# Output projection and tokens cut to 520 columns, w_out in sixteen single blocks split on GpSimd, a tenth expert weight buffer, and rows stored unscaled

## The reference, cut to what matters

```python
xn   = rmsnorm(x, norm_mix);  z, xbc, dt, u = split(xn @ w_in)
y_ssd = rmsnorm(ssd(conv(xbc), dt) * silu(z), ssd_norm)      # state-space heads, chunks of 128
y_s5  = s5(u); y_s5 = rmsnorm(gelu(y_s5) * sigmoid(gelu(y_s5) @ w_glu + b_glu), s5_norm)
x = x + concat([y_ssd, y_s5]) @ w_out
x = x + hier_moe(rmsnorm(x, norm_ffn))   # best of 4 groups, then best 2 of its 8 experts; SwiGLU of width 512
y_prompt = rmsnorm(x, norm_final)[:, N_META:]; y_sample = rmsnorm(x_sample, norm_final)
```

## Time and profile before

| | us |
|---|---|
| median of 3 runs | 1067.53 (1066.47 to 1075.4) |
| the profiled execution's own time | 1061.96 |
| its span | 1059.7 |
| first expert matmul | at 539.0 |
| last expert matmul ends | at 1036.3 |
| PE busy | 961.3 (91%) |
| DVE / ACT / POOL busy | 434.8 / 331.1 / 268.0 |
| granted TensorE clock, mean | 0.986 |

### The profile page before, as it was taken

How to read it: one execution, slowest core, us unless ns; L and a number is a source line. 1 busy time by engine, 2 the same in 40 slices (tenths; PEclk the granted TensorE clock), 3 DMA queues, 4 the chain that set the end, 5 groups by cost and what they waited for, 6 DMA issues and landing times.

```text
span 1059.7 us, 17219 instructions
## 1 busy us (share of the span) xinstructions
PE 961.3 (91%) x6496; PEld 682.0 (64%) x6497; DVE 434.8 (41%) x743; ACT 331.1 (31%) x662; POOL 268.0 (25%) x510
## 2 busy tenths in 40 slices
PE   6999999999999999999999999999877788998881
PEld 5889779877776788998765555555443444554440
DVE  6999877454466898951521111111100101111112
ACT  3025323453325784322422222232212121222113
POOL 1000888888421010000012222222222112222110
PEclk9999999999999999999999999999999999999996
DMA  7585172110098744255589999999999999999994
GB/s 268 125 142 92 29 121 81 41 63 22 12 223 226 254 147 175 87 238 239 218 323 392 396 383 398 385 394 397 395 396 395 396 413 404 409 410 408 425 385 167
DMA packets 73566, 277.54 MB, mean 262 GB/s; under 512 B 36953, under 2 KB 38873, under 8 KB 56497
## 3 DMA queue, kind: packets, MB, share of 16 engines
q1 hardware_dynamic: 63020, 252.67, 65.0%
q0 software_dynamic: 8720, 19.86, 6.8%
q10 hardware_dynamic: 1780, 4.41, 1.1%
HBM read 260.17 MB, written 25.61 MB: 270 GB/s over the span
## 4 chain that ended last, share of the span: by engine, by line
PE 68%; DMA 23%; DVE 5%; issue 2%; ACT 1%; POOL 0%; SPq 0%; ACTq 0%; POOLq 0%; DVEq 0%
PE ps L653 24%; DMA sb_arena<-w_up 20%; PE ps L1023 9%; PE ps L1037 7%; PE ps L1016 7%; PE ps L919 7%; PE ps L992 2%; DMA sb_arena<-ssm_in 2%; PE ps L685 1%; PE ps L741 1%; PE ps L798 1%; DVE sb_arena L1960 1%; PE ps L772 1%; PE ps L895 1%; PE ps L1030 1%
## 5 line engine op out<-in xcount | busy, mean ns | idle before, releaser
L653 PE MATMUL ps<-sb_arena 128*128 128x264 f32 (+1 forms) x1152 | 266.9, 392 | 9.1 <-DMA sb_arena<-wi 9.1
L653 PEld LDWEIGHTS ps<-sb_arena 128*128 128x128 f32 x1152 | 218.8, 191 | 57.5 <-DMA sb_arena<-wi 9.6
L1956 DVE TENSOR_TENSOR sb_s5b<-sb_s5b,ps 128x256 f32<-128x256 f32 x36 | 22.2, 617 | 408.0 <-PE ps L1023 408.0
L1023 PE MATMUL ps<-sb_arena 128*64 128x256 f32 x1152 | 131.3, 380 | 22.0 <-DMA sb_arena<-w_up 22.0
L1037 PE MATMUL ps<-sb_arena 128*64 128x512 f32 x576 | 131.5, 598 | 20.7 <-DVE sb_arena L1960 20.7
L1016 PE MATMUL ps<-sb_arena 128*64 128x256 f32 x1152 | 132.6, 383 | 16.5 <-DMA sb_arena<-w_gate 15.8
L1016 PEld LDWEIGHTS ps<-sb_arena 128*64 128x64 f32 x1152 | 83.6, 138 | 76.3 <-DMA sb_arena<-w_gate 27.0
L1023 PEld LDWEIGHTS ps<-sb_arena 128*64 128x64 f32 x1152 | 82.5, 137 | 67.1 <-DMA sb_arena<-w_up 28.9
L1388 ACT ACTIVATE sb_kxf<-ps,sb_gate_of 64x512 f32<-64x512 f32 x36 | 24.6, 683 | 301.1 <-PE ps L1037 301.1
L1037 PEld LDWEIGHTS ps<-sb_arena 128*64 128x64 f32 x576 | 39.0, 136 | 90.1 <-issue 60.9
L1415 DVE TENSOR_TENSOR sb_arena<-sb_arena 128x64 f32<-128x64 f32 (+12 forms) x86 | 78.0, 907 | 19.5 <-DMA sb_arena<-ssm_in 12.2
(11 more groups left out here) (308 smaller groups left out, 1210.3 us busy)
## 6 DMA issues: line engine op xcount, KB each, us to landing
sb_arena<-w_gate SPq DMA_DIRECT2D x32, 2048.0 KB, 33.7
sb_arena<-w_up SPq DMA_DIRECT2D x32, 2048.0 KB, 35.9
sb_arena<-w_down SPq DMA_DIRECT2D x32, 2048.0 KB, 35.6
sb_arena<-wi SPq DMA_DIRECT2D x28, 512.0 KB, 4.0
sb_arena<-w_out SPq DMA_DIRECT2D x4, 2048.0 KB, 8.5
sb_arena<-ssm_in POOLq DMA_DIRECT2D x8, 512.0 KB, 8.9
sb_arena<-wglu SPq DMA_DIRECT2D x8, 512.0 KB, 5.0
o_ssm_s<-sb_arena POOLq DMA_DIRECT2D x8, 512.0 KB, 4.0
```

The lines of the kernel that those rows point to most:

```text
L653: last = mm(ps[:, b0 + h, 0:t1 - t0], ring[w % 3][:, k, :], src[:, k, t0:t1], start=k == 0, stop=k == KD - 1)
L1023: last = mm(ps[64 * r:64 * r + 64, 1, 0:256], xt[:, k, :], Wu[s][:, k, 256 * r:256 * r + 256], start=k == 0, stop=k == KD - 1)
L1956: V.tensor_tensor(hh.rearrange("p (j c) -> p c j", j=2), sg.rearrange("p (c j) -> p c j", j=2), ps[:, 1, 0:256].rearrange("p (c j) -> p c ...
```

## The change

- All that is not part of a recurrence works on the 520 columns that are in the output: w = 20 to 35, the projection, the roots, the residual, the logits and the token rows (`NT`, `HALF`, `HALVES_T`, `TR`; the fifth token tile has 8 rows in place of 24).
- w_out comes in sixteen blocks of 128 columns through three buffers (`wo_load`, `next_wo`). ACT and DVE split blocks 0 and 1, POOL splits blocks 2 to 15, each when the block two before it is done on PE.
- The first expert's gate weight has a buffer of its own (`Wg_first`); Wg[0..2] take the gates of experts 1, 2, 3. Nine loads are issued earlier or in another order; `Wg[1]`, `Wu[2]` and `Wd[2]` go out as soon as the residual rows are there.
- Rows are stored unscaled to x_scr and sum_scr. The one-hot rows for the first tile carry the root, a second one-hot product gives a table of roots, and ACT's staging copy scales by it.
- `wide(25)` moves behind `ssd_c(2)` and `state_outputs(8, 8)`; h_done is set ahead of POOL's five sample instructions; small matmuls move between the eight k steps of `wide(17)`, `(18)`, `(19)` and `(30)`; `conv(9)` and the eviction of w = 18 move ahead of the decay sums; ring loads 26 and 27 go ahead of `y_store(0)`.
- The GELU reads its input with stride and writes in order, where it read in order and wrote with stride.
- SP waits for the scatters itself instead of for POOL.

```diff
+NT = N - META
+HALF = NT // 2
+HALVES_T = ((META, META + HALF), (META + HALF, N))
+TR = [(i * P, min(P, NT - i * P)) for i in range(5)]
...
+        wo = [part(14944 + 1024 * i, KD, P) for i in range(3)]
+        Wg_first = part(4096, KD, FF)
...
+            ring_load(26)
+            ring_load(27)
             y_store(0)
-            for w in range(26, 29):
-                ring_load(w)
+            ring_load(28)
...
+            sp.dma_start(Wu[1], usrc[1]).then_inc(wu_ld[1], 16)
+            def next_wo(o):
+                sp.wait_ge(o_mm, o - 2)
+                wo_load(o)
+            next_wo(3)
             sp.wait_ge(y2_done, 8)
+            sp.dma_start(Wg_first, gsrc[0]).then_inc(ld_x[0], 16)
+            for o in range(4, 7):
+                next_wo(o)
...
+            for o in range(7, 11):
+                next_wo(o)
             sp.dma_start(Wu[0], usrc[0]).then_inc(wu_ld[0], 16)
+            next_wo(11)
+            next_wo(12)
+            sp.dma_start(Wg[0], gsrc[1]).then_inc(wg_ld[0], 16)
+            next_wo(13)
+            next_wo(14)
             sp.dma_start(Wd_to[0], dsrc[0]).then_inc(wd_ld[0], 16)
+            next_wo(15)
+            sp.dma_start(Wg[2], gsrc[3]).then_inc(wg_ld[2], 16)
+            sp.wait_ge(o_mm, 16)
+            sp.dma_start(Wd_to[1], dsrc[1]).then_inc(wd_ld[1], 16)
+            sp.wait_ge(x1t_ev, 10)
+            for i, (t0, n) in enumerate(TR):
+                sp.dma_start(sum_scr[t0:t0 + n, :], x1[i][0:n]).then_inc(sum_st, 16)
+            sp.dma_start(Wg[1], gsrc[2]).then_inc(wg_ld[1], 16)
             sp.dma_start(Wu[2], usrc[2]).then_inc(wu_ld[2], 16)
+            sp.wait_ge(x1t_mm, 9)
             sp.dma_start(Wd_to[2], dsrc[2]).then_inc(wd_ld[2], 16)
...
             with sp.Fori(1, E_LOOP) as ep:
                 for s in range(WBUF):
                     e = ep * WBUF + s
+                    load_expert(s, of(usrc, e), of(dsrc, e), bass.ds(e - (WBUF - 1), 1))
+                    load_gate(s, of(gsrc, e + 1), bass.ds(e - (WBUF - 2), 1))
...
+            for o in range(2, 16):                        # POOL
+                pl.wait_ge(wo_ld[o % 3], 16 * (o // 3 + 1))
+                pl.wait_ge(o_mm, o - 1)
+                nc.gpsimd.tensor_copy(wo_hi[o % 2][:], wo[o % 3]).then_inc(wo_hid, 1)
+                pl.wait_ge(wo_hid, o + 1)
+                pl.wait_ge(wo_lod, o)
+                nc.gpsimd.tensor_tensor(wo_lo[o % 3][:], wo[o % 3], wo_hi[o % 2][:].bitcast(F32),
+                                        ALU.subtract).then_inc(wo_lod, 1)
...
-                    for h, (t0, t1) in enumerate(HALVES):
+                    for h, (t0, t1) in enumerate(HALVES if w < 20 else HALVES_T):
...
-            wide(25)
             pe.wait_ge(yo_ev, 4)
             state_outputs(0, 8)
             ssd_c(2)
             state_outputs(8, 8)
+            wide(25)
...
+                yh, yl, wh, wl = y_hi[o // 8], y_lo[o // 8], wo_hi[o % 2], wo_lo[o % 3]
+                pe.wait_ge(wo_lod, o + 1)
...
+            for j in range(10):
+                last = mm(ps[0:T, 5, T:T + IDXC], oh_row[:, j, :], oh_root[:, j, :], start=j == 0, stop=j == 9)
+            last.then_inc(tab_mm, 1)
...
-            for i, (t0, n) in enumerate(TT):                # ACT
-                act_(xs[i][0:n], x1[i][0:n], ACT.Copy, scale=ssum[0:n, i:i + 1]).then_inc(xs_done, 1)
-                ac.wait_ge(xs_done, i + 1)
-                ac.dma_start(x_scr[t0:t0 + n, :], xs[i][0:n, :]).then_inc(xs_st, 16)
+            for i, (t0, n) in enumerate(TR):
+                ac.dma_start(x_scr[t0:t0 + n, :], x1[i][0:n, :]).then_inc(xs_st, 16)
...
-                    act_(xst, xg[(u + 1) % RING], ACT.Copy).then_inc(staged, 1)
+                    act_(xst, xg[(u + 1) % RING], ACT.Copy, scale=root_of[:, bass.ds(q + 1, 1)]).then_inc(staged, 1)
...
-            wo_low(1)                                       # DVE, between project_out(1) and (2)
-            wo_low(2)                                       # between project_out(5) and (6)
-            wo_low(3)                                       # between project_out(9) and (10)
...
-            V.tensor_tensor(oh0, both[:, :, 0], both[:, :, 1], ALU.add).then_inc(hot_done, 1)
+            tt(oh0, both[:, :, 0], both[:, :, 1], ALU.add)
+            V.tensor_tensor(oh0, oh0, bc(ssum[:], 2, T), ALU.mult).then_inc(hot_done, 1)
...
+            tt(oh_root.rearrange("p (i k) t -> p i (k t)", k=2), oh_tile.rearrange("p (i k) t -> p i (k t)", k=2),
+               bc(ssum[:], 2, 2 * IDXC), ALU.mult)
```

More of the change, by code:

```diff
@@ L97, in build @@
         bc_scr = scratch("bc_scr", [NS, BCW])
-        x_scr = scratch("x_scr", [N, D])
-        sum_scr = scratch("sum_scr", [N, D])
+        x_scr = scratch("x_scr", [NT, D])
+        sum_scr = scratch("sum_scr", [NT, D])
         arena_at = -(-nc.sbuf_base // 32) * 32
@@ L186, in build @@
         Wd_to = [part(o + 8192, 2, 2 * D) for o in W_off]
-        xg = [part(4288 + 1024 * i, D, p=(0, T)) for i in range(RING)]
+        Wg_first = part(4096, KD, FF)
+        xg = [part(1024 * i, D, p=(0, T)) for i in range(RING)]
         xst = part(8384, D, p=(0, T))
@@ L190, in build @@
         ht = part(9920, 2, P)
-        Lt = part(4288, N, p=(0, 36))
-        xs = [part(o, D) for o in (4824, 5848, 6872, 19040, 20064)]
-        first = part(21088, D, p=(0, T))
+        Lt = part(9806, NT, p=(0, 36))
+        first = xst
+        root_of = part(10176, IDXC, p=(0, T))
         g8 = part(10344, KD)
-        rt = [8208]
+        rt = [8192]
         def small(*shape):
@@ L208, in build @@
         Ob = small(5 * E // 2).bitcast(BF16).rearrange("p (i e) -> p i e", e=E)
-        rm, m1, m2, r5, rdif = (small(5) for _ in range(5))
-        assert rt[0] <= 9920
+        rm, m1, m2, r5, rdif, valt = (small(5) for _ in range(6))
+        assert rt[0] <= 9806
         G = [part(10352 + 2048 * i, 2, D) for i in range(5)]
@@ L733, in _, with toeplitz_round @@
                 wide(w)
-            pe.wait_ge(t_ld, 16 * 32)
-            for rd in range(16):
+            def toeplitz_round(rd):
                 if rd >= 2:
@@ L828, in ssd_c @@
                 last.then_inc(st_mm, 1)
+            def ssd_c(c):
+                for i in range(8):
+                    ssd_y(c, i)
+                ssd_states(c)
             pe.wait_ge(de_in, 1)
@@ L869, in _ @@
             wide(29)
-            ssd_c(4)
-            for w in range(30, 36):
+            wide(30)
+            ssd_states(4)
+            for w in range(31, 36):
                 wide(w)
@@ L1207, in z_evac @@
                 b0 = wide_bank(w)
-                act_(zT[:, w - 20, 0:SPLIT], ps[:, b0, 0:SPLIT], ACT.Copy)
-                act_(zT[:, w - 20, SPLIT:N], ps[:, b0 + 1, 0:N - SPLIT], ACT.Copy).then_inc(wide_free[w % 2], 1)
+                for h, (t0, t1) in enumerate(HALVES_T):
+                    last = act_(zT[:, w - 20, t0:t1], ps[:, b0 + h, 0:HALF], ACT.Copy)
+                last.then_inc(wide_free[w % 2], 1)
             def b_tokens(c):
@@ L1631, in _ @@
             V.tensor_tensor(dE[0:16, 4, 2, :], dE[0:16, 4, 1, :], dE[0:16, 4, 0, :], ALU.subtract).then_inc(de_in, 1)
-            for i in range(9, XBC):
+            for i in range(10, XBC):
                 conv(i)
```

279 lines of the change are left out of this document (146 added, 133 removed).

## The result

| | before | after |
|---|---|---|
| median, us | 1067.0 (1065.4 to 1075.4, 4 runs) | 1092.4 (1092.0 to 1092.9, 4 runs) |
| span of the profiled execution | 1059.7 | 1090.2 |
| granted TensorE clock, mean | 0.986 | 0.966 |
| projection begins | 404.7 | 424.7 |
| first expert begins | 538.8 | 568.6 |

The change made the kernel slower: ratio 1.0222, 95% interval 1.0169 to 1.0276. That it is slower is clear; that it is slower by 2% or more isn't. Forecast were 1068 us and a range that ended at 1079. Of the 30.5 us between the spans, 29.8 lie ahead of the experts and 7.2 behind them, and the weight stream gives back 6.5. (The first expert is counted from its first matmul, 0.1 to 0.2 us ahead of the piece in the chain.)

A forecast was written before the change was run, and what follows sets the result against it. PE and DMA take turns and the weight stream sets the end. The first expert starts 10.4 us later and the stream gains 9.9, so 1067.5 + 0.5 = 1068 us, range 1051 to 1079.

The forecast's parts named there:

- The hold of DVE by POOL: Projection: POOL's splits for blocks 6, 7 and 8 hold DVE's two-input work, so block 7 starts 8.8 us late.
- DVE isn't held: Rival for the projection: DVE always goes first or POOL gives way; 1056 us, chance 0.30.
- POOL sets the pace: Rival for the projection: POOL's split is long enough to make project_block wait for wo_lod; 1076 us, chance 0.14.
- The columns of the `wide`s: Sixteen wides on PE: 520 columns in place of 536 save 0.216 us each, -3.5 us.
- Routing: Ahead of the first expert: one more table of one-hot products and DVE's new product, +1.7 us, bounds +1.2 and +2.5.
- The clock behind block 7's wait: Projection: PE's idle ahead of block 7 brings slow matmuls at half clock, +1.7 us, bounds 0 and 4.
- The GELU was put at 0: ACT's GELU with the stride on the reading side takes as long as before: 0, bounds -0.5 and +1.2 each.
- Order of work up to the projection: Moving wide(25) makes PE wait up to 4 us, about half regained ahead of wide(28): +1.7 us, bounds 0 and +5.
- The small matmuls moved into the `wide`s run as they did: Small matmuls between the wides' k steps cost nothing, as PE issues them all the same: 0.
- The stream: Weight loads from the first expert on: 1.7 fewer loads left, -8.9 us; fewer rows -0.7; SP's scatter wait -0.3.
- S: Shift of the first expert's start, the sum of all terms ahead of it: +10.4 us.
- The head start is not kept: Rival for the stream: DMA is left without a free buffer, so the tenth buffer buys nothing; 1078 us, chance 0.06.

The follow-up runs named there:

- e4_dve: Changed kernel with DVE's project_out(5) ahead of the low parts and project_out(6) among them; 1085.1 us.
- e6_lock: Changed kernel without POOL's subtractions for blocks 5 to 8, where PE uses the high part in place of the low one; 1088.5 us.
- e8_all: Changed kernel with the edits of e1_w25, e3_inter, e4_dve, e5_c4 and e7_tail together; 1057.6 us.
- e1_w25: Changed kernel with wide(25) back in its old place, ahead of the first state_outputs; 1085.3 us.
- e3_inter: Changed kernel with the small matmuls taken out of wide(17), wide(18) and wide(19) again; 1089.3 us.
- e5_c4: Changed kernel with ssd_y(4) taken out of wide(30) and set ahead of it with ssd_states(4), as ssd_c(4); 1083.2 us.
- e7_tail: Changed kernel with ACT's and POOL's tile loops written for 34 tiles, so no empty turns; 1084.9 us.
- e10_nine: Kernel of e8_all with the load of w_down of expert 2 held until the first expert's gate product is done; 1056.4 us.
- e11: Kernel of e8_all with the sum_scr stores and the three loads behind them held until the first tile is turned on PE; 1069.4 us.

## Why the prediction was wrong

**Right.** The hold of DVE by POOL and its place in DVE's order (e4_dve, e6_lock); the rival "DVE isn't held" falls, and so does "POOL sets the pace": PE never waits for POOL, and a copy that isn't held takes 1.04, forecast 1.0. The columns of the `wide`s: the first of them took 7.39 and takes 7.18 in e8_all, times 16 is 3.4 (3.5). Routing: 24.8 from the projection's end to the first expert before, 26.8 after, +2.0 (1.7). The clock behind block 7's wait: the block takes 7.17 where an unhindered one takes 5.74, +1.4 (1.7).

**Right by two things that cancel.** The GELU was put at 0, and from the first GELU to the end of `wide(28)`, whose k steps need one each, 10.3 us pass in place of 10.2. ACT in the kernel before, then in the changed one:

```profile
338.64 1.17 ACT L1240 ACTIVATE sb_arena<-sb_arena 128x528 f32<-128x528 f32 x1
...
339.67 1.14 ACT L1240 ACTIVATE sb_arena<-sb_arena 128x528 f32<-128x528 f32 x1
```
```profile
348.52 1.13 ACT L1312 ACTIVATE sb_arena<-sb_arena 128x512 f32<-128x512 f32 x1
...
349.66 1.12 ACT L1312 ACTIVATE sb_arena<-sb_arena 128x512 f32<-128x512 f32 x1
```

One GELU is a little shorter, but the next begins 1.14 us behind it in place of 1.03 (1.13 and 1.02 in the mean). Against that, a wait of 0.58 for the load between the fourth and the fifth is gone. The new stride is the likely cause of the slower pace; no run put the old one back. PE's wait of 0.85 ahead of `wide(28)` costs nothing by itself, since the last GELU sets the end.

**Right with luck.** That the wait of 8.79 is the forecast's 8.8 is chance. The subtractions held DVE for 7.2 us (4.51 - 2.31 and 11.27 - 6.23 with e6_lock), forecast 6.6; the copies for 0.8, forecast 2.7, as the one at 456.77 came second and was held itself. And 8.8 was to be block 7's delay, not PE's wait: counted from the projection's start block 7 begins at 52.2 in place of 44.1, 8.1 later, where the forecast's terms up to there make some 9.5.

**Wrong, by size.** "Order of work up to the projection ... +1.7, bounds 0 and +5": 6.6 by e1_w25. The waits, 2.5 us in all, lie in what was forecast ("waits up to 4 us"). But the step priced the clock for block 7 alone, from a stretch of 3.4 us, and took nothing for it here, where some 14 us at half clock followed waits of 0.8 and 1.8. It also took half of the wait back at the GELU ahead of `wide(28)`. Nothing came back there: PE's wait ahead of `wide(28)` is 0.85, and it is 0.86 with `wide(25)` in its old place (e1_w25). The projection's columns gave 3.0, forecast 1.3: a block that waits for nothing took 5.93 and takes 5.74, sixteen times 0.19.

**Wrong, by a step not followed.** This is the step that failed the forecast: "The small matmuls moved into the `wide`s run as they did, 0, as PE issues them all the same." Two things were in this sentence, and a third stood beside it.
- In `wide(17)` to `(19)` they don't run as they did: 3.1 to 3.5 us (e3_inter).
- In `wide(30)` the last product of `ssd_y(4)` comes 9 us later, and I asked what it costs PE and not who waits for it: DVE's chunk 4, the state, SP's wait with three loads behind it, the sample states, ACT's sigmoids. 9.3 us (e5_c4), the largest single loss. The rule was in front of me for block 7 (what is queued behind the waiting instruction) and was not applied to this move.
- ACT's exponential behind the silu cost PE another 1.5 us of waiting at 216; it had no term at all.

**Wrong, at the end.** The tail had no term. The tile counts stood in the working (36, then 34), but not that the loops round up to fours: 7.6 us (e7_tail), most of it POOL's DRAIN behind its two empty turns.

**The stream.** Forecast -9.9 with the rows and SP's wait, measured -6.5 in the changed kernel and -7.9 in e8_all (-5.5 to -8.4 in nine profiles with this stream). The sign and the fullness of DMA are right; the way to count, 1.7 loads at 5.2 us, is not: e10_nine holds a load and loses 1.2 at most. The bytes say the same: at a mean of 398 GB/s in both, the changed kernel moves 191.7 MB from the first expert to the start of the last `up` and the kernel before 194.4, so 2.7 MB less, or 6.8 us, where the forecast's 1.7 loads and the rows make 3.8 MB.

So the terms that were priced come to -3.4 (`wide`s) - 3.0 (projection) + 6.6 (order) + 8.8 (block 7) + 0.6 (block 2, less two short waits of before) + 1.4 (clock) + 2.0 (routing) = 13.0 us, not far from S = 10.4. What was put at nothing, or had no term, is 9.3 + 3.5 + 1.5 = 14.3. That leaves 2.5 of the 29.8. Part of it is clock that no repair brought back: in e5 and e8 to e11 `wide(30)` takes 8.9 to 10.1 us, with half clock in it, where a `wide` of this width takes 7.2. The rest the runs don't separate, and the profiles differ by 1 to 2 us among themselves. Behind the experts 7.2 came that had no term either. The signs of being right were met at block 7 and missed at the first expert: 5 to 14 us late were named, 29.8 it is. None of the rivals was this one. "The head start is not kept", at 1078, was the nearest in time and wrong in cause.
